# The last stage of a one-layer kernel: splits and gate copies reordered, and all four token tiles' outputs added by VectorE instead of two by an adding transfer

## What is computed

```python
ff = jnp.square(jax.nn.relu(jnp.einsum('bsd,df->bsf', hn, w_up[i])))
h = h + rms_norm(jnp.einsum('bsf,fd->bsd', ff, w_down[i]), mlp_post_g[i])
gate = jax.nn.sigmoid(jnp.einsum('bsd,de->bse', h, w_ple_gate[i]) + b_ple_gate[i])
ple = jnp.einsum('bsp,pd->bsd', p[i], w_ple[i]) * gate
h = h + rms_norm(ple, ple_post_g[i])
```

## Time and profile before

| | before |
|---|---|
| median of 3 runs | 585.18 us (585.04 to 585.37) |
| the profiled execution | 586.4 us |
| its span | 584.7 us |
| TensorE busy | 569.1 us, 97% |
| VectorE busy | 501.1 us, 86% |
| ScalarE busy | 374.9 us, 64% |
| GpSimd busy | 114.2 us, 20% |
| granted TensorE clock, mean | 0.991 |

### The profile page before, as it was taken

The page is one execution under the profiler, slowest core; times in us unless marked ns, Lnnn a source line. Parts: engine busy times, 40 slices in busy tenths (PEclk is TensorE's granted clock), DMA queues, the critical chain, the costliest instruction groups (busy, mean ns, idle before and its releaser), DMA issues.

```text
span 584.7 us, 8927 instructions
## 1 busy us (share of the span) xinstructions
PE 569.1 (97%) x3364; PEld 496.0 (85%) x3364; DVE 501.1 (86%) x637; ACT 374.9 (64%) x595; POOL 114.2 (20%) x165
## 2 busy tenths in 40 slices
PE   9999999999999999999999999999999999999991
PEld 7888888888888888989999999999999999887881
DVE  5899895788676997999989999999899999787975
ACT  6886765785546646657665665666556655775862
POOL 0331536000104372101010011010100110123114
PEclk9999999999999999999999999999999999999996
DMA  8981008224003649377484592774754927877946
GB/s 270 372 309 62 0 5 321 73 72 143 3 1 109 243 173 298 78 228 188 89 256 106 143 253 44 246 161 90 242 121 112 281 40 214 242 234 141 288 128 140
DMA packets 28747, 95.30 MB, mean 163 GB/s; under 512 B 3232, under 2 KB 5664, under 8 KB 28320
## 3 DMA queue, kind: packets, MB, share of 16 engines
q1 hardware_dynamic: 20448, 67.64, 32.5%
q0 software_dynamic: 6672, 20.71, 20.6%
q10 hardware_dynamic: 1584, 6.37, 2.8%
HBM read 86.85 MB, written 7.34 MB: 161 GB/s over the span
## 4 chain that ended last, share of the span: by engine, by line
PE 77%; DVE 9%; DMA 6%; ACT 4%; POOL 2%; issue 2%; SPq 0%; DVEq 0%; ACTq 0%; POOLq 0%
PE psum L2694 24%; PE psum L2698 23%; PE psum L2699 23%; DMA ple_spill<-ple 2%; DVE up_lo L1078 2%; PE psum L2932 2%; DMA raw_second<-weights_dram 2%; PE psum L2912 1%; PE psum L2749 1%; DMA raw<-weights_dram 1%; ACT junk_late L1596 1%; DVE ple L1172 1%; DMA first_raw_a<-weights_dram 1%; PE psum L2763 1%; DVE t_lo L1223 1%
## 5 line engine op out<-in xcount | busy, mean ns | idle before, releaser
L2694 PE MATMUL psum<-t_hi,a_hi 128*128 128x512 f32 x216 | 85.0, 393 | 0.5 <-DVE acc L1282 0.5
L2698 PE MATMUL psum<-t_lo,a_hi 128*128 128x512 f32 x216 | 84.6, 392 | 0.0
L2699 PE MATMUL psum<-t_hi,a_lo 128*128 128x512 f32 x216 | 84.1, 389 | 0.0
L2694 PE MATMUL psum<-w_hi,actT_hi 128*128 128x512 f32 (+1 forms) x178 | 69.7, 392 | 0.0
L2699 PE MATMUL psum<-w_hi,actT_lo 128*128 128x512 f32 (+1 forms) x178 | 68.5, 385 | 0.0
L2698 PE MATMUL psum<-w_lo,actT_hi 128*128 128x512 f32 (+1 forms) x178 | 68.5, 385 | 0.0
L2698 PE MATMUL psum<-sum_lo,up_hi 128*128 128x256 f32 x224 | 63.4, 283 | 0.0
L2699 PE MATMUL psum<-sum_hi,up_lo 128*128 128x256 f32 x224 | 63.4, 283 | 0.0
L2694 PE MATMUL psum<-sum_hi,up_hi 128*128 128x256 f32 x224 | 63.2, 282 | 0.0
L2429 POOL DMA_DIRECT2D raw_x<-weights_dram x21 | 18.5, 882 | 216.1 <-DVE t_lo L1223 215.8
L2699 PE MATMUL psum<-actT_hi,up_lo 128*128 128x256 f32 (+1 forms) x200 | 60.0, 300 | 0.0
(11 more groups left out here) (298 smaller groups left out, 1453.7 us busy)
## 6 DMA issues: line engine op xcount, KB each, us to landing
raw<-weights_dram SPq DMA_DIRECT2D x40, 512.0 KB, 4.6
raw_o<-weights_dram SPq DMA_DIRECT2D x23, 512.0 KB, 4.4
raw_x<-weights_dram POOLq DMA_DIRECT2D x21, 512.0 KB, 5.5
raw_second<-weights_dram SPq DMA_DIRECT2D x16, 512.0 KB, 4.1
raw_x<-weights_dram SPq DMA_DIRECT2D x9, 512.0 KB, 6.2
qk_raw<-weights_dram SPq DMA_DIRECT2D x8, 512.0 KB, 6.7
raw_o<-weights_dram POOLq DMA_DIRECT2D x7, 512.0 KB, 6.9
raw_second<-weights_dram POOLq DMA_DIRECT2D x6, 512.0 KB, 7.7
```

Of the source, the lines that this page charges most:

```text
L2694: begin = nc.tensor.matmul(out, a_hi, b_hi, start=first, stop=False, skip_group_check=read_between)
L2698: nc.tensor.matmul(out, a_hi, b_lo, start=False, stop=False, skip_group_check=read_between)
L2699: return nc.tensor.matmul(out, a_lo, b_hi, start=False, stop=last, skip_group_check=read_between)
```

## The change

Four things are changed, all at the end of the program. (1) On ScalarE, the second part of T2's high split goes behind the copy of C11, the copies of h2T 4 and 5, the two bias seeds and the split of E; the seeds go behind those copies too. On VectorE, T2's second low split goes behind the sums and the split of E. (2) ADDED_IN_OUT is gone: all nine gate tiles get a gain_ple and an add_ple, add_ple now works on one gate tile, and SyncE stores each of them from h. The early store of h for tokens 2 and 0 and GpSimd's adding transfers are gone. (3) ScalarE's end runs one sigmoid ahead of the squares. (4) GpSimd's loop is written out, with a place of its own for each token's partial sum, so that partial sums 0, 1 and 4 are made as soon as they can be.

```diff
@@ -289,7 +289,6 @@
 GATE_TILES = ((0, 0, W), (1, 0, W), (2, W, W), (2, 0, W), (3, W, W), (0, W, W), (3, 0, W),
               (1, W, W // 2), (1, W + W // 2, W // 2))
 TOKENS_DONE = (2, 0, 3, 1)
-ADDED_IN_OUT = (2, 0)
 
...
@@ -1453,26 +1452,15 @@
                                         ).then_inc(pl_gained, 1)
 
 
-            def add_ple(t):
-
-                tiles = gate_tiles_of(t)
-                if t in ADDED_IN_OUT:
-                    dve.wait_ge(pl_rstd, TOKENS_DONE.index(t) + 1)
-                    for i in tiles:
-                        dve.wait_ge(pl_gated, i + 1)
-                        cut = slice(GATE_TILES[i][1], GATE_TILES[i][1] + GATE_TILES[i][2])
-                        nc.vector.scalar_tensor_tensor(out=ple_of(t)[:, cut], in0=acc[:, t, cut],
-                                                       scalar=rstd_pl[:, t:t + 1], in1=ple_gain[:, cut],
-                                                       op0=ALU.mult, op1=ALU.mult).then_inc(out_ready, 1)
-                    return
-                gain_ple(tiles[-1])
+            def add_ple(i):
+
+                t, c0, width = GATE_TILES[i]
+                cut = slice(c0, c0 + width)
                 dve.wait_ge(pl_rstd, TOKENS_DONE.index(t) + 1)
-                dve.wait_ge(pl_gained, GAINED.index(tiles[-1]) + 1)
-                for i in tiles:
-                    cut = slice(GATE_TILES[i][1], GATE_TILES[i][1] + GATE_TILES[i][2])
-                    nc.vector.scalar_tensor_tensor(out=h[:, t, cut], in0=ple_of(t)[:, cut],
-                                                   scalar=rstd_pl[:, t:t + 1], in1=h[:, t, cut],
-                                                   op0=ALU.mult, op1=ALU.add).then_inc(out_ready, 1)
+                dve.wait_ge(pl_gained, GAINED.index(i) + 1)
+                nc.vector.scalar_tensor_tensor(out=h[:, t, cut], in0=ple_of(t)[:, cut],
+                                               scalar=rstd_pl[:, t:t + 1], in1=h[:, t, cut],
+                                               op0=ALU.mult, op1=ALU.add).then_inc(out_ready, 1)
 
             def tail_down(d):
 
...
@@ -1500,11 +1488,11 @@
             h2_split_lo(3)
             add_mlp(3)
             gate_split_lo(GATE_T2, 0)
-            gate_split_lo(GATE_T2, 1)
             h2_sum(OF_E, 0)
             h2_sum(OF_S2, 0)
             h2_sum(OF_S3, 0)
             h2_sum_split_lo(OF_E, 0)
+            gate_split_lo(GATE_T2, 1)
             h2_sum_split_lo(OF_S2, 0)
             gate_split_lo(GATE_T3, 0)
             h2_split_lo(5)
@@ -1527,22 +1515,33 @@
             h2_sum_split_lo(OF_S4, 1)
             gate_ple(0)
             gate_ple(1)
+            gain_ple(0)
             gate_fold(1)
             gate_ple(2)
+            gain_ple(1)
             gate_ple(3)
-            gain_ple(1)
             gate_c22(1)
+            gain_ple(2)
+            gain_ple(3)
             add_ple(2)
+            add_ple(3)
             gate_ple(4)
+            gain_ple(4)
             gate_ple(5)
-            gain_ple(4)
+            gain_ple(5)
             add_ple(0)
+            add_ple(5)
             gate_ple(6)
+            gain_ple(6)
             gate_ple(7)
-            add_ple(3)
             gain_ple(7)
+            add_ple(4)
             gate_ple(8)
+            add_ple(6)
+            gain_ple(8)
             add_ple(1)
+            add_ple(7)
+            add_ple(8)
 
 
 
...
@@ -2251,14 +2250,14 @@
             square_down(3)
             gate_split_hi(GATE_T2, 0)
             gate_copy(COPY_C11, 0)
-            gate_split_hi(GATE_T2, 1)
-            seed_e(0)
-            seed_e(1)
             gate_copy(COPY_C11, 1)
             h2_copy_raw(4)
             h2_copy_raw(5)
             h2_split_hi(5)
+            seed_e(0)
+            seed_e(1)
             h2_sum_split_hi(OF_E, 0)
+            gate_split_hi(GATE_T2, 1)
             h2_sum_split_hi(OF_S2, 0)
             gate_split_hi(GATE_T3, 0)
             h2_copy_raw(6)
@@ -2287,9 +2286,16 @@
             sigmoid(3)
             square_ple(2)
             square_ple(3)
-            for i in range(4, len(GATE_TILES)):
-                sigmoid(i)
-                square_ple(i)
+            sigmoid(4)
+            sigmoid(5)
+            square_ple(4)
+            sigmoid(6)
+            square_ple(5)
+            sigmoid(7)
+            square_ple(6)
+            sigmoid(8)
+            square_ple(7)
+            square_ple(8)
 
 
...
@@ -2497,34 +2503,39 @@
             add_s4(0)
             add_s4(1)
 
-            for n, t in enumerate(TOKENS_DONE):
-                *before, last_tile = gate_tiles_of(t)
-                total = D * EPS
-                for place_in_row, i in enumerate(before):
-                    partial = ple_tmp[:, place_in_row:place_in_row + 1]
-                    pool.wait_ge(pl_squared, i + 1)
-                    after(nc.gpsimd.tensor_scalar(partial, ss_pl[:, i:i + 1], total, None, ALU.add))
-                    total = partial
+            def partial_sum(i):
+
+                t = GATE_TILES[i][0]
+                partial = ple_partial[:, t:t + 1]
+                before = partial if i != gate_tiles_of(t)[0] else D * EPS
+                pool.wait_ge(pl_squared, i + 1)
+                after(nc.gpsimd.tensor_scalar(partial, ss_pl[:, i:i + 1], before, None, ALU.add))
+
+            def ple_rstd(t):
+
+                last_tile = gate_tiles_of(t)[-1]
+                mean = ple_mean
+                pool.wait_ge(pl_squared, last_tile + 1)
                 if last_tile == LAST_GATED:
-
-                    nc.gpsimd.tensor_tensor(last_gated[:, width_of(LAST_GATED):], total, plus_half, ALU.pow
-                                            ).then_inc(root_ready, 1)
-                    pool.wait_ge(pl_squared, last_tile + 1)
                     mean = ss_pl[:, last_tile:last_tile + 1]
                 else:
-                    pool.wait_ge(pl_squared, last_tile + 1)
-                    mean = ple_tmp[:, 2:3]
-                    after(nc.gpsimd.tensor_scalar(mean, ss_pl[:, last_tile:last_tile + 1], total,
+                    after(nc.gpsimd.tensor_scalar(mean, ss_pl[:, last_tile:last_tile + 1], ple_partial[:, t:t + 1],
                                                   1.0 / D, ALU.add, ALU.mult))
                 nc.gpsimd.tensor_tensor(rstd_pl[:, t:t + 1], mean, minus_half[:, 0:1], ALU.pow
                                         ).then_inc(pl_rstd, 1)
-                pool.wait_ge(pl_rstd, n + 1)
-                if t in ADDED_IN_OUT:
-                    if n == 0:
-                        pool.wait_ge(late_added, s4_added)
-                        pool.wait_ge(stored, 16 * len(ADDED_IN_OUT))
-                    pool.wait_ge(out_ready, 2 * (n + 1))
-                    nc.gpsimd.dma_start(out[t * P:(t + 1) * P], ple_of(t), accum_op=ALU.add).then_inc(late_added, 16)
+                pool.wait_ge(pl_rstd, TOKENS_DONE.index(t) + 1)
+
+            partial_sum(0)
+            partial_sum(1)
+            partial_sum(2)
+            ple_rstd(2)
+            partial_sum(4)
+            ple_rstd(0)
+            ple_rstd(3)
+            partial_sum(7)
+            nc.gpsimd.tensor_tensor(last_gated[:, width_of(LAST_GATED):], ple_partial[:, 1:2], plus_half, ALU.pow
+                                    ).then_inc(root_ready, 1)
+            ple_rstd(1)
 
 
 
@@ -2666,20 +2677,13 @@
             gate_x(GATE_22, 1)
             sp.dma_start(ple_late[1][:], ple_spill[:, 2:4, :]).then_inc(ple_loaded[1], 16)
             sp.dma_start(ple_gain[:], rows["gate"][:, 1, :]).then_inc(post_loaded, 16)
-            for t in ADDED_IN_OUT:
-                sp.wait_ge(h2_ready, t + 1)
-                sp.dma_start(out[t * P:(t + 1) * P], h[:, t, :]).then_inc(stored, 16)
-            sp.wait_ge(stored, 16 * len(ADDED_IN_OUT))
-            order = [i for t in TOKENS_DONE for i in gate_tiles_of(t)]
+            order = (2, 3, 0, 5, 4, 6, 1, 7, 8)
             for n, i in enumerate(order):
                 t, c0, width = GATE_TILES[i]
-                if t in ADDED_IN_OUT:
-                    continue
                 sp.wait_ge(out_ready, n + 1)
                 sp.dma_start(out[t * P:(t + 1) * P, c0:c0 + width], h[:, t, c0:c0 + width]
                              ).then_inc(stored, 16)
-            sp.wait_ge(late_added, s4_added + 16 * len(ADDED_IN_OUT))
-            sp.wait_ge(stored, 16 * (len(ADDED_IN_OUT) + len(order) - 2 * len(ADDED_IN_OUT)))
+            sp.wait_ge(stored, 16 * len(order))
 
 
```

More of the change, by code:

```diff
@@ L481, in hymba_layer @@
         ss_pl, rstd_pl = stat[:, 146:], stat[:, 64:68]
-        ple_tmp = stat[:, 56:59]
+        ple_partial, ple_mean = stat[:, 56:60], stat[:, 61:62]
         plus_half = stat[:, 60:61]
@@ L1440, in gate_ple @@
                 nc.vector.tensor_tensor(gated, acc[:, t, cut], ple_of(t)[:, cut], ALU.mult).then_inc(pl_gated, 1)
-            GAINED = (1, 4, 6, 7, 8)
+            GAINED = tuple(range(len(GATE_TILES)))
             def gain_ple(i):
```

## The result

The changed kernel took **589.95 us** (median of 4 runs, 588.81 to 590.04), the kernel before 585.27 beside it (4 runs, 585.04 to 585.86). The ratio is 1.0074, with a 95% interval of 1.0056 to 1.0091. The forecast was 582.3 and its range ended at 584.0. The profiled execution of after took 590.04 us for a span of 588.3.

What follows compares the result with a forecast made beforehand. The prediction took TensorE, busy 97%, as the bound, so time could come only from gaps in its work or the tail after its last matmul. It summed -1.65 - 1.73 + 0.5 = -2.9 us to 582.3 us, range 581.2 to 584.0.

Steps and rivals of the forecast that it cites:

- The step that failed: Weight transfers onto h2T_a: T4 lands at 550.6, S4 at 553.4 and 554.8, 0.5 us late; 0.25 us booked.
- signs of failure: New TensorE gap at 543 to 560, ScalarE standing over 1 us at S4's or T4's split, GpSimd sums above 0.9 us.
- The rival of the weight queue: Weight transfers, issued later beside the ple_late_a load, keep part of the advance: 583.3, up to 584.0 us; chance 0.14.
- The slower rival: ScalarE stands at S4's split because T4 takes over 11.3 us; 585.9 us if T4 takes 12 us; chance 0.04.
- Part one, the gap: ScalarE's reordering at 534 to 545 closes TensorE's 1.90 us gap, less 0.25 for late transfers: -1.65 us.
- both are wanted 1.9 us earlier, at 549.2: ScalarE's need for T4 and the last S4 sum moves from 551.13 and 556.24 to 549.2 and 554.3.
- Part two, the tail: Ledger from VectorE's first multiply to the end, after TensorE's last matmul: +0.90 - 0.64 - 0.93 - 1.06 = -1.73 us.
- VectorE's hold: Packed VectorE work delays GpSimd's sums for tokens 2 and 3, between 0 and 1.14 us; 0.5 us booked.
- Multiply 0 to 4: Start of the tail on VectorE: 6.68 us before, 7.58 forecast with gains 0 and 1 ahead of multiply 3, +0.90.
- Token 3's first add to token 1's: Late tail: 3.76 us before, 2.70 forecast with one partial sum left ahead of the root, bounds 2.25 and 2.88, -1.06.
- every one of GpSimd's sums would be held, and the time 582.9: Tail: by the rule that GpSimd contends with two-input VectorE instructions, all its sums are delayed, giving 582.9 us.
- The rival "VectorE's density": Tail: both sums and the partial sum held, gain 3 no longer hidden, 0.64 and 0.6 us more, 583.5 us; chance 0.10.

Runs made afterwards that it cites:

- loads_held: The changed kernel with SyncE's loads of ple_gain and ple_late_b issued only after both S4 adding transfers have landed; 585.25 us, ratio 0.9994 to the kernel before.
- s4_on_vector: The changed kernel with the sum S4 made by two VectorE additions in place of the two adding transfers; 584.52 us, ratio 0.9975 to the kernel before.
- tail_alone: The changed kernel with the old order around T2's second part, so only the new tail; 585.81 us, ratio 0.9994 to the kernel before.
- t2_sooner: The changed kernel with T2's second split right behind bank 5's copies and its low part behind E's sum; 586.39 us, ratio 1.0007 to the kernel before.
- s4_again: The same kernel as s4_on_vector, word for word, timed again beside adds_behind_root; 584.38 us, ratio 0.9981 to the kernel before.
- order_s4_vector: The kernel before, old tail, with the new order around T2's second part and S4 summed on VectorE; 585.09 us, ratio 0.9990 to the kernel before.
- means_on_vector: s4_on_vector with four means and partial sum 7 moved from GpSimd to VectorE, and square(8) without the root; 584.64 us, ratio 0.9976 to the kernel before.
- adds_behind_root: s4_on_vector with VectorE waiting for GpSimd's root before the adds of tiles 4 and 6; 583.60 us, ratio 0.9972 to the kernel before.

## Why the prediction was wrong

**The step that failed** is "With T4 again 8.6 us after its issue it lands at 550.6, the others 2.8 and 4.2 us behind", which booked 0.25 us for the whole transfer queue. The prediction's own signs of failure came with it: a TensorE gap that begins before 560 (559.17), and ScalarE at rest for more than 1 us at S4's split (3.86) and at T4's (2.11). T4 itself was nearly right, 9.2 us. The 4.2 us behind it was not: S4 took 8.3, and in loads_held, with nothing changed but the loads, it took 4.4. I moved SyncE's loads forward with "everything else comes 1.9 us sooner", and then priced the transfers as if the queues beside them stood where they had stood. The rival of the weight queue (0.14) named ple_late_a as neighbour; the ones that met S4 were ple_late_b and ple_gain, of which no part of the prediction speaks.

**The slower rival** had the place and the mechanism, ScalarE standing still at S4's split, but a wrong way in ("T4 would have to take 11.3 us") and so 0.04. S4 landed at 559.5, 5.2 us after it was wanted. Its price was also missing a part: I counted the wait alone, and not the lower clock behind it.

**What the gap then cost**, by TensorE from raw_second's issue to the last matmul: 43.99 us before, 49.07 after, 5.08 more. That is -1.89 for the old gap, +4.53 for the new one, and 12 matmuls at 0.43 in place of 0.23, +2.4; together +5.04. VectorE, which sets the end, sees less: multiply 0 comes 3.50 us later (564.00 - 528.00 against 560.74 - 528.24), and the tail from there takes 21.79 us against 21.36, 0.43 more; together 3.93, which is the last add's 57.79 less 53.86 in the table. The medians differ by 4.68. Before's profiled execution, 586.4, lay 1.1 us above the median beside it and after's at its own, so that some 0.8 us of the difference of medians is in no trace here.

The lower clock made VectorE and ScalarE wait for TensorE in two places, here VectorE's and ScalarE's rows of after:

```profile
569.12 0.69 DVE L1416 TENSOR_TENSOR acc<-acc,psum 128x512 f32<-128x512 f32 x1 [0.76 <-PE psum L2703]
...
576.85 1.42 DVE L1461 SCALAR_TENSOR_TENSOR h<-ple_late_a,stat,h 128x512 f32<-128x512 f32 x2 [1.86 <-POOL stat L2524]
```

```profile
574.52 0.60 ACT L2219 ACTIVATE acc<-psum 128x512 f32<-128x512 f32 x1 [0.82 <-PE psum L2703]
```

The wait at gate_c22 (569.12) cost nothing in the end: while VectorE stood still, GpSimd's mean of token 2 took 0.27 us and not the 0.93 of s4_on_vector, and token 2's adds begin 6.93 us behind multiply 0 in after and 6.91 in s4_on_vector. The other wait reached the end. ScalarE waits for the product under sigmoid 6 until 574.52 and then squares tile 5, so multiply 5 (573.58) to token 0's add (576.85) takes 3.27 us; in s4_on_vector, at full clock, it takes 2.56. That is 0.71 us; without it the tail is 21.08, as in the kernels with the new tail and the full clock (21.07 or 21.08 in tail_alone, s4_on_vector, t2_sooner and s4_again; loads_held has 21.29, since multiply 2 stood 0.2 us for its ple_late_b).

**Part one, the gap.** The mechanism and its 1.90 us were right at the place itself, 1.89 measured. But its 1.65 us would not have arrived either. In the six kernels of the table with the new order and no collision (loads_held, s4_on_vector, order_s4_vector, means_on_vector, adds_behind_root, s4_again) multiply 0 stands 8.84 to 8.88 us behind T4's high split, whenever that is, and ScalarE waits 1.5 to 2.3 us for T4 in each. So T4's landing sets the tail's start: issued 2.0 us later than before, it gives 0.3 to 1.1 us for landings of 9.4 to 8.6 us. I had written "both are wanted 1.9 us earlier, at 549.2", let T4 land at 550.6, and then charged S4's 0.5 us alone. By 550.6 + 8.84 = 559.4 multiply 0 comes 1.3 us sooner than 560.74, so the term was 0.6 and not 0.25 even by my own landing.

**Part two, the tail**, was forecast at -1.73, +0.5 for VectorE's hold, and measured at 21.07 - 21.36 = -0.29. VectorE's timeline of s4_on_vector carries the ledger:

```profile
559.56 1.29 DVE L1448 TENSOR_TENSOR acc<-acc,ple_late_a 128x512 f32<-128x512 f32 x2
...
567.80 0.68 DVE L1448 TENSOR_TENSOR acc<-acc,ple_late_b 128x512 f32<-128x512 f32 x1
...
569.13 0.68 DVE L1448 TENSOR_TENSOR acc<-acc,ple_late_a 128x512 f32<-128x512 f32 x1
...
571.69 1.41 DVE L1470 SCALAR_TENSOR_TENSOR h<-ple_late_a,stat,h 128x512 f32<-128x512 f32 x2 [1.16 <-POOL stat L2532]
573.03 0.68 DVE L1448 TENSOR_TENSOR acc<-acc,ple_late_b 128x512 f32<-128x512 f32 x1
...
575.67 0.75 DVE L1470 SCALAR_TENSOR_TENSOR h<-ple_late_b,stat,h 128x512 f32<-128x512 f32 x1 [0.45 <-POOL stat L2532]
...
579.09 1.54 DVE L1470 SCALAR_TENSOR_TENSOR h<-ple_late_a,stat,h 128x512 f32<-128x512 f32 x3 [1.34 <-POOL stat L2532]
```

- Multiply 0 to 4: 8.24, forecast 7.58. The mean of token 2 took 0.93 us under gains 2 and 3. That alone is the 0.66.
- Multiply 4 to 5: 1.33, forecast 1.32. Multiply 5 to 6: 3.90, forecast as before, 3.91 (573.29 - 569.38).
- Multiply 6 to token 3's first add: 2.64, forecast 2.58; the adding transfer's 0.92 us is gone as said.
- Token 3's first add to token 1's: 3.42, forecast 2.70, and even my bound from above was 2.88. I kept one partial sum at 0.88, but with VectorE packed it took 1.10 and the root 0.92 instead of 0.61.

So VectorE's density cost 0.66 + 0.06 + 0.72 = 1.44 us in place of 0.5. The case stood in the prediction ("every one of GpSimd's sums would be held, and the time 582.9"), and it was nearer. My forecast allowed two holds of 0.57 and left the root and the partial sum ahead of it out of the count, though the earlier trace rows already had a partial sum at 0.88. The rival "VectorE's density" had this partial sum; it booked 1.24 us on top of the forecast where 0.94 came, but half of it for gain 3, which still fits (the two gains end at 565.73, the adds begin at 566.47). adds_behind_root shows the last hold, of partial sum and root, by taking it away; that of token 2's mean rests on the rows alone.

Taken together, after's trace is 6.8 us off the forecast of -2.9: 5.15 of it in part one (+3.50 for -1.65), 0.94 in part two by VectorE's density, and 0.71 in part two by the lower clock.

**What stays open.** That engines alternate between the two queues by packet fits the packet counts of after (76 and 76, 69 and 69, 44 and 41, 42 and 46 in the four us from 552), but nothing here tells it from another way of sharing. In tail_alone, with S4 still on its way, GpSimd's queue passed 13 packets against 128 from 554 to 556; whether only a few of the 16 DMA engines had any of it left isn't shown. What makes T4 take 8.6 us in one trace, 9.4 in another of the same kernel (s4_again, s4_on_vector), and 10.7 in tail_alone isn't settled; ple_late_b and ple_gain aren't the reason, since it took 9.2 in loads_held as well.

## What to carry to other kernels

A gap closed in one place moved the later issues forward here, on SyncE's queue too, but not the transfers that hang on the step that was put back. Write out both lists of issue times for the new kernel and see what is now in flight together; a landing time read from the old trace holds only for the neighbours it had. Where a transfer of small pieces stands on the path and an engine has a us to spare, do the sum on the engine: here that took the ratio from 1.0074 to 0.9975. And where GpSimd's small operations are on the path, leave VectorE at rest for them: a wait added on VectorE shortened the tail by 0.9 us.
